# Two RMS norms between two transformer blocks, folded into one scale per token that is applied behind the projections

## The chip, the cores and the metric

One core of a Trainium2 chip (trn2). The program computes two layers in one launch; the metric is the device time of that launch in microseconds, as the median of several runs. Inputs are in the chip's memory in layouts that the host made ahead; the output is a 256 x 1024 array of float32.

## The reference, cut to what matters

```python
# end of the first block, with x of shape (256, 1024)
x = x + conv_glu_ffn(rms_norm(x, ffn_norm_g), w_up, ffn_conv_w, w_down)
x = rms_norm(x, final_norm_g)                  # first norm between the blocks
...
# start of the second block: 16 meta tokens stand ahead of the 256
xn = rmsnorm(concat([meta_tokens, x]), norm1_g)   # second norm
proj = xn @ w_in_2                             # 12 column blocks first: 8 for xm, 4 for the state space branch
xm -> causal conv of 4 taps -> silu -> block diagonal q, k;  xm -> block diagonal v
...
x = x + mixer output                           # the residual is the output of the first norm
```

Both norms are y = x * rsqrt(mean(x^2) + eps) * g, over the 1024 channels of a token. x is kept transposed: 128 partitions hold channels, 8 tiles k of 128 channels each, tokens are the columns (256, or 272 with the meta tokens).

## The kernel before, in words

The kernel is written straight for the engines: every engine has its own program, a stage is a block with a barrier of all engines at its end, and semaphores order the work inside a block. Weights come as a stream of 512 KB pieces (128 partitions x 1024) that SyncE loads into a ring of 8 slots; a slot is loaded again once TensorE has told `used` for it.

**Split products.** The projections in question run in three passes of a fast format. ScalarE rounds a ring slot to its high part (`part_high`, L247 to L249), VectorE subtracts that from the slot and leaves the low part in the slot's place (`part_low`, L251 to L254), and TensorE multiplies high by high, high by low and low by high (`three`, L256 to L260). The activations are split in the same way. A product of one 128-column block is 8 x 3 matmuls of 272 tokens.

**The stages around the change**, in order:

1. The feed-forward block (L1022 to L1173). Banks 0 to 3 of PSUM gather x plus the down projection. At its end VectorE waits for TensorE's last product (L1120), copies the four banks to x (L1122), and the block ends.
2. `rms_norm` of x with final_norm_g into `xin` (L1182). ScalarE squares four tiles and VectorE the other four, VectorE adds them in pairs, TensorE sums over the partitions with a matrix of ones (L288, 4 matmuls), VectorE makes mean + eps and its reciprocal (L305, L307), ScalarE the root (L282), VectorE scales the 8 tiles (L310).
3. `rms_norm` of xin, now with the 16 meta tokens, into `h` (L1193). The same steps again; beside it ScalarE rounds the first three ring slots.
4. The large block of the second layer (L1274 on). ScalarE rounds h in two halves (L1543), VectorE subtracts (L1332) and then makes the low parts of the slots; TensorE runs the 12 products (L1648) in banks 0 to 3, in turn; ScalarE copies each out of its bank (L1547) and rounds the slot three ahead (L1546); from the fifth slot on VectorE also runs the 4-tap convolution of a finished tile after each low part (`conv`, L1319 to L1327: 4 linked operations). Then TensorE goes on with plain float32 projections of h (`z_products`, L1249, one of 8 matmuls each, in banks 0 and 1 at first), the block diagonal products (L1655 to L1671) and the heads; VectorE goes on with the state space parameters (from L1342), which need exp(log_dt) from ScalarE (L1552), the heads and the scans. GpSimd clears `k0` (L1292), copies xin to x for the residual (L1293) and later multiplies in eight rounds, one per scan pair (L1301 to L1305). The block ends with 6 plain projections (L1785) on TensorE.

Each engine works in its own program order: a wait in VectorE's list holds all that stands behind it.

Of the kernel before, what the change touches and what calls it, by code (L numbers as in the profile page):

```python
# [104 lines left out]
def build(nc, out, stream, x_t, meta_t, cols, first, second, last, keep):  # L105
    with ExitStack() as ctx:
# [28 lines left out]
        spare = sb("spare", [P, 1])  # L135
        arena, arena_parts = split_place("arena", [P, 38912], ARENA_PARTS)
# [126 lines left out]
        normed = {"n": 0}  # L263

        def rms_norm(src, dst, gain, eps, squares, width=T, beside=None):


            n = normed["n"]
            normed["n"] += 1
            sq, total, mean, root = S("norm_squares"), S("norm_total"), S("norm_mean"), S("norm_root")  # L270
            with nc.Block() as block:
# [13 lines left out]
                def _(pe):  # L285
                    for k in range(4):
                        pe.wait_ge(sq, n * 4 + k + 1)
                        mm = nc.tensor.matmul(bank[7][:, 0:width], ones, squares[:, 4 + k, 0:width],  # L288
                                              start=k == 0, stop=k == 3)
# [698 lines left out]
        xin = a6.take(KT, TT)  # L988
        sq2 = a6.take(KT, TT)
# [24 lines left out]
        def ff_low(dve, n, i=0):  # L1014
# [6 lines left out]
                 beside=(lambda act: [ff_high(act, n) for n in (-4, -3)], lambda dve: [ff_low(dve, n) for n in (-4, -3)]))  # L1021
        with nc.Block() as block:  # L1022
            @block.sync
            def _(sp):
                sp.dma_start(xin[:, :, 0:M], meta_t).then_inc(S("meta_in"), 16)
# [52 lines left out]
            def _(dve):  # L1078
# [41 lines left out]
                dve.wait_ge(used[FF_LAST[1]], before[FF_LAST[1]] + 1)  # L1120
                for b in range(4):
                    ins = v.tensor_copy(x[:, 2 * b:2 * b + 2, :], b3(b))  # L1122
                    ins.then_inc(drained[b], 1)
                for b in range(4):
                    dve.wait_ge(drained[b], pe_at.banks[b] + 2)

            @block.scalar
            def _(act):
# [17 lines left out]
                for j in range(2):  # L1146
                    silu(pairs, j)

# [36 lines left out]
        xp = Area(arena_parts[25344])  # L1185
        xn_block, xn_high, xn_low = xp.take(4, D), xp.take(KT, TT), xp.take(KT, TT)
        xn_filled = [pe_at.rounds[s] + 1 for s in range(4)]

        def xn_part_high(act, n, i=0):
            if not (isinstance(i, int) and i * 4 + n >= 12):  # L1190
                part_high(act, xn_block, n % 4, i + (n // 4 + xn_filled[n % 4]))

        rms_norm(lambda k: xin[:, k, :], lambda k: h[:, k, :], "norm1_g_2", RMS_EPS, squares_b, TT,  # L1193
# [1398 lines left out]
```

## Time and profile before

| | us |
|---|---|
| median of 3 runs (lowest, highest) | 1820.93 (1820.82, 1825.67) |
| the profiled execution's own time | 1822.69 |
| its span | 1820.9 |
| mean granted TensorE clock, share of full speed | 0.956 |

Times in rows are microseconds from the start of the span, unless marked ns. PE is TensorE's matmuls, PEld its weight loads, DVE VectorE, ACT ScalarE, POOL GpSimd; L12 is line 12 of the kernel. A float32 matmul in full precision leaves two matmul records in the trace, one of the fast format leaves one.

### The profile page before, as it was taken

To read this page: it belongs to the slowest core of one execution; us is meant where nothing else is said; L and a number is where in the kernel's file an instruction comes from. 1 tells how busy PE (TensorE), PEld (TensorE's weight loads), DVE (VectorE), ACT (ScalarE), POOL (GpSimd) and SP (SyncE) were. 2 spreads that over 40 slices of the span, in tenths; PEclk is the share of its full clock that TensorE was granted. 3 is DMA by queue.
4 is the path that set the end of the run, shared out by engine and by line. 5 is a ranking of instruction groups with operands and counts; after the bars stand their busy time and mean duration, and the time that the engine had idled before them with its cause. 6 is when DMAs were issued, how large, how long until landed. Compare 5 with 4: busy or idle time off the path is not lost. (4 is left out here: it accounts for less than half of the span.)

```text
span 1820.9 us, 32801 instructions
## 1 busy us (share of the span) xinstructions
PE 1677.4 (92%) x11170; PEld 1517.9 (83%) x11170; DVE 1152.2 (63%) x2268; ACT 794.7 (44%) x1326; POOL 333.6 (18%) x205
## 2 busy tenths in 40 slices
PE   5989898779999499999969998999999999999997
PEld 4968897669999396777859998999999988888886
DVE  4464312847676674662445999777775477777776
ACT  3441112225553265223324554455555555555554
POOL 0030000404444000221727697000000000000000
PEclk8989899889999699899979999999999999999999
DMA  6403123324554141114434667555556776666663
GB/s 229 175 24 104 58 82 127 117 90 178 185 186 171 62 172 70 35 47 150 155 100 137 202 217 204 169 175 174 178 178 205 237 235 238 232 232 233 237 232 127
DMA packets 93700, 289.44 MB, mean 159 GB/s; under 512 B 11328, under 2 KB 27968, under 8 KB 93248
## 3 DMA queue, kind: packets, MB, share of 16 engines
q1 hardware_dynamic: 93200, 287.61, 46.2%
q10 hardware_dynamic: 432, 0.90, 0.2%
q8 instruction: 45, 0.74, 0.2%
q14 instruction: 23, 0.19, 0.0%
HBM read 270.64 MB, written 17.83 MB: 158 GB/s over the span
## 5 line engine op out<-in xcount | busy, mean ns | idle before, releaser
L258 PE MATMUL psum<-arena_parts 128*128 128x256 f32 (+2 forms) x1664 | 483.3, 290 | 59.9 <-DVE ring_parts L253 24.1
L260 PE MATMUL psum<-arena_parts,ring_parts 128*128 128x256 f32 (+1 forms) x1600 | 455.6, 285 | 0.0
L2380 DVE TENSOR_TENSOR ring_parts<-ring,arena_parts 128x512 fp32r<-128x512 f32 x434 | 293.4, 689 | 132.4 <-ACT arena_parts L2200 104.6
L258 PEld LDWEIGHTS psum<-arena_parts 128*128 128x128 f32 x1664 | 320.8, 193 | 64.3 <-issue 29.0
L259 PE MATMUL psum<-h_parts,arena_parts 128*128 128x256 f32 x1152 | 325.2, 282 | 0.0
L260 PEld LDWEIGHTS psum<-arena_parts,ring_parts 128*128 128x128 f32 x1600 | 308.5, 193 | 0.0
L253 POOL TENSOR_TENSOR ring_parts<-ring,arena_parts 128x1024 fp32r<-128x1024 f32 x79 | 208.5, 2655 | 319.6 <-ACT arena_parts L249 265.6
L259 PEld LDWEIGHTS psum<-h_parts,arena_parts 128*128 128x128 f32 x1152 | 219.4, 190 | 0.0
L229 PE MATMUL psum<-h,ring 128*128 128x256 f32 x896 | 212.2, 397 | 0.0
L2169 PE MATMUL psum<-arena_parts,x_parts 128*128 128x512 f32 x512 | 202.9, 396 | 2.7 <-DVE x_parts L2407 2.7
L2171 PE MATMUL psum<-arena_parts,x_parts 128*128 128x512 f32 x512 | 202.7, 396 | 0.0
L2170 PE MATMUL psum<-ring_parts,x_parts 128*128 128x512 f32 x512 | 200.9, 392 | 0.0
L229 PEld LDWEIGHTS psum<-h,ring 128*128 128x128 f32 x896 | 176.2, 200 | 28.9 <-issue 2.7
L2200 ACT ACTIVATE arena_parts<-ring 128x512 fp32r<-128x512 f32 x217 | 136.4, 629 | 124.1 <-PE psum L2171 96.8
L2197 ACT ACTIVATE arena_parts<-ring 128x512 fp32r<-128x512 f32 x217 | 136.6, 630 | 76.1 <-PE psum L2171 58.8
L259 PE MATMUL psum<-arena_parts 128*128 128x256 f32 (+1 forms) x448 | 130.3, 291 | 0.0
L2169 PEld LDWEIGHTS psum<-arena_parts,x_parts 128*128 128x128 f32 x512 | 95.7, 187 | 25.9 <-DVE ring_parts L2380 2.9
L1017 DVE TENSOR_TENSOR ring_parts<-ring,arena_parts 128x1024 fp32r<-128x1024 f32 x66 | 84.0, 1277 | 52.6 <-ACT arena_parts L1012 47.9
L2170 PEld LDWEIGHTS psum<-ring_parts,x_parts 128*128 128x128 f32 x512 | 96.3, 188 | 23.5
L2171 PEld LDWEIGHTS psum<-arena_parts,x_parts 128*128 128x128 f32 x512 | 95.7, 187 | 24.1
L249 ACT ACTIVATE arena_parts<-ring 128x1024 fp32r<-128x1024 f32 x76 | 79.3, 1053 | 56.1 <-DMA ring<-stream 56.0
L1051 PE MATMUL psum<-arena_parts 128*128 128x256 f32 x352 | 100.2, 285 | 2.8 <-DVEq L1101 2.8
(486 smaller groups left out, 2903.1 us busy)
## 6 DMA issues: line engine op xcount, KB each, us to landing
ring<-stream SPq DMA_DIRECT2D x473, 512.0 KB, 3.6
kept<-arena SPq DMA_DIRECT2D x128, 128.0 KB, 2.0
arena<-kept SPq DMA_DIRECT2D x32, 512.0 KB, 4.7
arena<-first SPq DMA_DIRECT2D x1, 2144.0 KB, 7.7
arena<-second SPq DMA_DIRECT2D x1, 1632.0 KB, 7.1
x<-x_t SPq DMA_DIRECT2D x1, 1024.0 KB, 5.8
out<-arena SPq DMA_DIRECT2D x4, 256.0 KB, 2.1
arena<-last ACTq DMA_DIRECT2D x1, 512.0 KB, 3.4
```

The source lines that it names most:

```text
L229: mm = nc.tensor.matmul(b[:, 0:width], w[:, k, :], h[:, k, lo:lo + width], start=k == 0, stop=k == KT - 1)
L253: ns.tensor_tensor(low[:, s, :], ring[:, s, :], high[:, s, :].bitcast(F32), ALU.subtract)\
L258: nc.tensor.matmul(dst, stationary[0], moving[0], start=first, stop=False)
L259: nc.tensor.matmul(dst, stationary[0], moving[1], start=False, stop=False)
L260: return nc.tensor.matmul(dst, stationary[1], moving[0], start=False, stop=last_one)
L1051: mm(b, high[:, s, w], h_high[:, k, :], start=k == 0, stop=False)
L2169: mm(b, gate_high[:, q % 4, t], expert_high[:, m % 2, w], start=False, stop=False)
L2170: mm(b, gate_high[:, q % 4, t], low[:, s, w], start=False, stop=False)
L2171: ins = mm(b, gate_low[:, q % 4, t], expert_high[:, m % 2, w], start=False, stop=last_one)
L2197: nc.scalar.activation(expert_high[:, m % 2, halves[0]], ring[:, s, halves[0]], ACT.Copy)\
L2200: nc.scalar.activation(expert_high[:, m % 2, halves[1]], ring[:, s, halves[1]], ACT.Copy)\
L2380: v.tensor_tensor(low[:, s, w], ring[:, s, w], expert_high[:, m % 2, w].bitcast(F32), ALU.subtract)\
```

## The change

- The feed-forward block no longer waits for the last product on VectorE and copies nothing out. In its place VectorE prepares small tables: `both_g` = final_norm_g * norm1_g, the meta tokens times norm1_g, their squares, and `sums_of`, a stationary matrix per tile whose left 64 columns are final_norm_g^2 + eps and whose right 64 columns are ones; ScalarE and VectorE split the first three ring slots there.
- Both calls of `rms_norm` are gone. In the large block ScalarE makes the high part of x * both_g straight from the PSUM banks and VectorE the low part, bank by bank; the first product waits for each bank's parts (tiles 0 and 1, then 2 and 3, ...).
- Behind that VectorE copies the banks to x, ScalarE squares x (4 operations), and after the third product TensorE sums the squares: 8 matmuls of 16 columns for the meta tokens, 8 of 256 columns with `sums_of`. Rows 0 to 63 of the sum give the joint scale of both norms, rows 64 to 127 that of the first norm alone. VectorE and ScalarE make the inverse root once, TensorE spreads row 0 over all partitions (one matmul, after the fourth product), ScalarE copies it to `scale`.
- The products run in seven banks (4, 5, 6, 0, 1, 2, 3, ...). VectorE takes each out of its bank times `scale` (`take`), in an order written out by hand among the low parts and convolutions; 8 operations that write the scaled h stand behind the last low part. Before the first plain projection TensorE waits for these 8.
- The residual is scaled late: one more matmul spreads row 64 (`scale_1`), ScalarE copies it, and GpSimd multiplies x by it and by final_norm_g, 16 operations behind its eight rounds.

```diff
@@ the feed-forward block, VectorE @@
-                dve.wait_ge(used[FF_LAST[1]], before[FF_LAST[1]] + 1)
-                for b in range(4):
-                    ins = v.tensor_copy(x[:, 2 * b:2 * b + 2, :], b3(b))
-                    ins.then_inc(drained[b], 1)
-                for b in range(4):
-                    dve.wait_ge(drained[b], pe_at.banks[b] + 2)
+                gain_1, gain_2 = (par[:, at[n]:at[n] + KT] for n in ("final_norm_g", "norm1_g_2"))
+                dve.wait_ge(S("meta_in"), 16)
+                v.tensor_tensor(both_g, gain_1, gain_2, ALU.mult)
+                v.tensor_tensor(meta_g, meta, gain_2.unsqueeze(2).broadcast_to([P, KT, M]), ALU.mult)
+                v.tensor_tensor(meta_squares, meta, meta, ALU.mult)
+                vec.link(v.tensor_tensor(both_square, gain_1, gain_1, ALU.mult))
+                vec.link(v.tensor_scalar(both_square, both_square, RMS_EPS, None, ALU.add))
+                v.tensor_copy(sums_of[:, :, 0:64], both_square.unsqueeze(2).broadcast_to([P, KT, 64]))
+                v.tensor_copy(sums_of[:, :, 64:P], ones[:, 0:64].unsqueeze(1).broadcast_to([P, KT, 64]))
+                v.memset(eps_row[0:64, :], RMS_EPS * RMS_EPS)
+                v.memset(eps_row[64:P, :], RMS_EPS)
+                for n in range(AHEAD):
+                    part_low(dve, nc.vector, xn_block, n, split["blocks"] + 3 * FT + n + 1)
@@ ScalarE @@
+                for n in range(AHEAD):
+                    xn_part_high(act, n)
@@ between the blocks @@
-        rms_norm(lambda k: x[:, k, :], lambda k: xin[:, k, M:TT], "final_norm_g", RMS_EPS, squares_b := sq2)
-        rms_norm(lambda k: xin[:, k, :], lambda k: h[:, k, :], "norm1_g_2", RMS_EPS, squares_b, TT, ...)
@@ the large block, GpSimd @@
-                poo.tell(g.tensor_copy(x[:], xin[:, :, M:TT]), x_kept, ONCE + 1)
...
+                pool.wait_ge(k0_ready, ONCE + 1)
+                for k in range(KT):
+                    ins = g.tensor_tensor(x[:, k, :], x[:, k, :], scale_1[:], ALU.mult)
+                poo.link(ins)
+                for k in range(KT):
+                    ins = g.tensor_scalar(x[:, k, :], x[:, k, :], col("final_norm_g", k), None, ALU.mult)
+                poo.link(ins)
@@ VectorE @@
+                def take(n):
+                    evacuate(dve, [n % 4], [P_BANKS[n]], 1, lambda q, b, i: v.tensor_tensor(
+                        both[:, n, :], b[:, 0:TT], scale[:, 0:TT], ALU.mult))
...
+                for b in range(4):
+                    dve.wait_ge(S("h_rounded"), split["h"] + b + 1)
+                    if b == 0:
+                        v.tensor_tensor(xn_low[:, :, 0:M], meta_g, xn_high[:, :, 0:M].bitcast(F32), ALU.subtract)
+                    for k in (2 * b, 2 * b + 1):
+                        ins = v.scalar_tensor_tensor(xn_low[:, k, M:TT], x_half(k), both_g[:, k:k + 1],
+                                                     xn_high[:, k, M:TT].bitcast(F32), ALU.mult, ALU.subtract)
+                    ins.then_inc(S("h_parts"), 1)
+                for b in range(4):
+                    v.tensor_copy(x[:, 2 * b:2 * b + 2, :], b3(b)).then_inc(drained[b], 1)
+                next_low(3); next_low(4)
+                dve.wait_ge(S("norm_total"), n_norm + 1)
+                v.tensor_scalar(roots[:, 0:M], bank[7][:, 0:M], 1.0 / D, RMS_EPS, ALU.mult, ALU.add)
+                vec.link(v.tensor_scalar(roots[:, M:TT], bank[7][:, M:TT], 1.0 / D, eps_row, ALU.mult, ALU.add))
+                vec.tell(v.reciprocal(roots[:], roots[:]), S("norm_mean"), n_norm + 1)
+                next_low(5)
+                dve.wait_ge(scales_made, ONCE + 1)
+                take(0);  next_low(6);  conv(0)
+                take(1);  next_low(7);  conv(1)
+                take(2);  next_low(8)
+                take(3);  conv(2);  next_low(9)
+                take(4);  conv(3);  next_low(10)
+                take(5);  next_low(11)
+                for k in range(KT):
+                    ins = v.scalar_tensor_tensor(h[:, k, M:TT], x[:, k, :], both_g[:, k:k + 1], scale[:, M:TT],
+                                                 ALU.mult, ALU.mult)
+                ins.then_inc(h_scaled, 1)
+                take(6);  conv(4);  take(7);  conv(5);  take(8);  take(9)
+                conv(6);  take(10);  take(11);  conv(7)
@@ ScalarE @@
-                for n in range(12):
-                    if n + AHEAD < 12:
-                        xn_part_high(act, n + AHEAD)
-                    evacuate(act, [n % 4], [n % 4], 1, lambda q, b, i: a.activation(both[:, n, :], b[:, 0:TT], ACT.Copy))
-                    if n >= 6:
-                        silu(n - 6)
+                a.activation(xn_high[:, :, 0:M], meta_g, ACT.Copy)
+                for k in range(KT):
+                    ins = a.activation(xn_high[:, k, M:TT], bank[k // 2][:, k % 2 * T:(k % 2 + 1) * T], ACT.Identity,
+                                       scale=both_g[:, k:k + 1])
+                    if k % 2:
+                        ins.then_inc(S("h_rounded"), 1)
+                xn_part_high(act, 3)
+                for b in range(4):
+                    act.wait_ge(drained[b], free_at[b])
+                    ins = a.activation(x_squares[:, 2 * b:2 * b + 2, :], x[:, 2 * b:2 * b + 2, :], ACT.Square)
+                    if b % 2:
+                        ins.then_inc(S("norm_squares"), 1)
+                xn_part_high(act, 4)
+                a.activation(spare[:], ones[:, 0:1], ACT.Sqrt)
+                act.wait_ge(S("norm_mean"), n_norm + 1)
+                a.activation(roots[:], roots[:], ACT.Sqrt).then_inc(S("norm_root"), 1)
+                xn_part_high(act, 5)
+                act.wait_ge(scale_spread, ONCE + 1)
+                sca.tell(a.activation(scale[:, 0:TT], bank[7][:, 0:TT], ACT.Copy), scales_made, ONCE + 1)
+                for n in range(6, 12):
+                    xn_part_high(act, n)
+                    if n >= 8:
+                        silu(n - 8)
+                for c in range(4, 6):
+                    silu(c)
@@ TensorE @@
-                    project(pe, [n % 4], [n % 4], 1, product(n))
+                    project(pe, [n % 4], [P_BANKS[n]], 1, product(n))
+                    if n == 2:
+                        for k in range(KT):
+                            mm(bank[7][:, 0:M], ones, meta_squares[:, k, :], start=k == 0, stop=k == KT - 1)
+                        for k in range(KT):
+                            if k % 4 == 0:
+                                pe.wait_ge(S("norm_squares"), normed["squares"] + k // 4 + 1)
+                            ins = mm(bank[7][:, M:TT], sums_of[:, k, :], x_squares[:, k, :], start=k == 0, stop=k == KT - 1)
+                        ins.then_inc(S("norm_total"), 1)
+                    if n == 3:
+                        pe.wait_ge(S("norm_root"), n_norm + 1)
+                        mm(bank[7][:, 0:TT], ident[:, 0:1].broadcast_to([P, P]), roots[:], start=True, stop=True)\
+                            .then_inc(scale_spread, 1)
...
+                pe.wait_ge(h_scaled, ONCE + 1)
                 z_products(pe, 2)
...
+                mm(bank[4][:, T:2 * T], ident[:, 64:65].broadcast_to([P, P]), roots[:, M:TT], start=True, stop=True)
```

In the diff above, calls of one line that stand under each other in VectorE's list are written side by side.

## Rows read from the trace of the kernel before

**Rows 1.** The page: busy time of each engine, share of the span, instructions.
```profile
PE 1677.4 (92%) x11170; PEld 1517.9 (83%) x11170; DVE 1152.2 (63%) x2268; ACT 794.7 (44%) x1326; POOL 333.6 (18%) x205
```
**Rows 2.** Timeline of TensorE: start, duration, line, shapes, count, [idle before <-releaser].
```profile
589.96 0.28 PE L1065 MATMUL psum<-arena_parts,ring_parts 128*128 128x256 f32 x1
...
624.51 0.57 PE L258 MATMUL psum<-arena_parts 128*128 128x272 f32 x1 [12.79 <-DVE ring_parts L253]
...
662.32 7.07 PE L229 MATMUL psum<-h,ring 128*128 128x256 f32 x32
...
836.29 14.08 PE L229 MATMUL psum<-h,ring 128*128 128x256 f32 x64
```
**Rows 3.** Timeline of VectorE between the two blocks.
```profile
590.27 2.48 DVE L1122 COPY x<-psum 128x512 f32<-128x512 f32 x4 [6.21 <-PE psum L1065]
593.39 1.43 DVE L296 TENSOR_TENSOR arena<-x 128x256 f32<-128x256 f32 x4 [0.64 <-PEq L1022]
...
601.92 3.26 DVE L310 SCALAR_TENSOR_TENSOR arena<-x,par,scale 128x256 f32<-128x256 f32 x8 [0.55 <-ACT scale L282]
...
612.23 1.85 DVE L307 RECIPROCAL scale<-scale 128x272 f32<-128x272 f32 x1
...
623.15 4.62 DVE L253 TENSOR_TENSOR ring_parts<-ring,arena_parts 128x1024 fp32r<-128x1024 f32 x4
```
**Rows 4.** Timeline of ScalarE from the feed-forward block's end to the first reload.
```profile
584.15 0.42 ACT L1131 ACTIVATE arena<-arena 128x256 f32<-128x256 f32 x1 [3.53 <-DVEq L1101]
...
614.12 0.43 ACT L282 ACTIVATE scale<-scale 128x272 f32<-128x272 f32 x1 [4.12 <-DVE scale L307]
...
629.66 0.40 ACT L1547 ACTIVATE arena<-psum 128x272 f32<-128x272 f32 x1 [8.06 <-PE psum L260]
633.41 1.06 ACT L249 ACTIVATE arena_parts<-ring 128x1024 fp32r<-128x1024 f32 x1 [3.35 <-DMA ring<-stream]
```
**Rows 5.** Windows: length; busy PE, PEld, DVE, ACT, POOL; clock; DMA; GB/s.
```profile
624.50:626.50 2.00, 1.99 (x9) 2.00 (x10) 2.00 (x2) 0.00 (x0) 0.00 (x0) 0.50 0.02 7
...
630.50:662.00 31.50, 31.50 (x255) 31.50 (x255) 24.47 (x40) 14.54 (x24) 0.00 (x0) 1.00 0.63 227
```
**Rows 6.** Timeline of TensorE: two other short stops in the program.
```profile
353.58 0.58 PE L258 MATMUL psum<-arena_parts 128*128 128x256 f32 x1 [2.41 <-DVE arena_parts L976]
...
871.78 3.72 PE L1821 MATMUL psum<-arena,ring 128*128 128x256 f32 x16 [2.26 <-DVE arena L1880]
```
**Rows 7.** Timeline of TensorE: small float32 matmuls of the large block.
```profile
716.48 1.95 PE L1697 MATMUL psum<-cst,arena 128*128 128x128 f32 x16
```
**Rows 8.** Timeline of VectorE: convolution, low part, a product read from PSUM.
```profile
645.25 0.41 DVE L1321 TENSOR_SCALAR arena<-arena,par 128x272 f32<-128x272 f32 x1
645.70 1.57 DVE L1325 SCALAR_TENSOR_TENSOR arena<-arena,par 128x271 f32<-128x271 f32 x3
647.31 1.22 DVE L253 TENSOR_TENSOR ring_parts<-ring,arena_parts 128x1024 fp32r<-128x1024 f32 x1
...
821.15 0.44 DVE L1449 TENSOR_TENSOR arena<-psum,arena 128x272 f32<-128x272 f32 x1 [1.84 <-PE psum L1725]
```
**Rows 9.** Timelines: VectorE's first parameter operation, TensorE's stop before the heads.
```profile
664.86 0.18 DVE L1342 TENSOR_TENSOR arena<-par,arena 128x16 f32<-128x16 f32 x1 [4.79 <-ACT arena L1552]
...
720.21 0.73 PE L1708 MATMUL psum<-cst,arena 4*16 4x4 f32 x6 [0.99 <-DVE arena L1426]
```
**Rows 10.** Timeline of GpSimd: its last operation of the large block.
```profile
828.64 0.73 POOL L1305 TENSOR_TENSOR arena<-arena 128x258 f32<-128x258 f32 x1
```
**Rows 11.** Groups of GpSimd by line and shape: busy, mean ns | idle before.
```profile
L1301 POOL TENSOR_TENSOR arena<-arena 128x258 f32<-128x258 f32 x8 | 5.9, 732 | 176.7 <-DVE arena L1468 167.1 <-issue 9.7
L509 POOL TENSOR_SCALAR arena<-arena,par 128x256 f32<-128x256 f32 x4 | 4.4, 1090 | 0.4
L506 POOL TENSOR_TENSOR arena<-arena 128x256 f32<-128x256 f32 x2 | 3.9, 1931 | 107.2 <-POOLq L359 107.1
```
**Rows 12.** One line of GpSimd: durations in ns, min/median/max, first and last start.
```profile
L1160 POOL TENSOR_TENSOR arena<-arena x22: 731/1105/1387, 413.2 to 584.6; 128x256 f32<-128x256 f32 x22
```

More of the change, by code:

```diff
@@ L1181, in build @@
                     tiles.banks[b] += 1
-        rms_norm(lambda k: x[:, k, :], lambda k: xin[:, k, M:TT], "final_norm_g", RMS_EPS, squares_b := sq2)
[L1185 to L1193, printed above, removed]
-                 beside=(lambda act: [xn_part_high(act, n) for n in range(AHEAD)], lambda dve: None))
+        n_norm = normed["n"]
+        normed["n"] += 1
         a7 = Area(arena, a6.at)
@@ L1216, in build @@
         k0 = r1.take(4, P)
-        assert r1.at <= a6.at
+        x_squares = Area(arena, 18560).take(8, T)
+        P_BANKS = (4, 5, 6, 0, 1, 2, 3, 4, 5, 6, 0, 1)
+        both = arena[:, a6.at:a6.at + 12 * TT].rearrange("p (c t) -> p c t", t=TT)
+        assert r1.at <= 4992
         a8 = Area(arena, a7.at)
@@ L1270, in build @@
         bt_re, bt_im = (bt[:, n, :].rearrange("p (c n) -> p c n", c=4) for n in range(2))
-        free_at = [ev_at.banks[n] + 1 for n in range(4)]
+        free_at = [ev_at.banks[n] + 1 for n in range(7)]
         projected = pe_at.rounds[3] + 3
+        k0_zeroed = poo.n + 1
         with nc.Block() as block:
@@ L1327, in conv, with x_half @@
                         vec.link(ins) if back < 3 else vec.tell(ins, S("ml_conv"), c + 1)
-                for half in range(2):
-                    k = slice(4 * half, 4 * half + 4)
-                    dve.wait_ge(S("h_rounded"), split["h"] + half + 1)
-                    v.tensor_tensor(xn_low[:, k, :], h[:, k, :], xn_high[:, k, :].bitcast(F32), ALU.subtract)\
-                        .then_inc(S("h_parts"), 1)
-                for n in range(12):
-                    part_low(dve, nc.vector, xn_block, n % 4, split["blocks"] + n + 1)
-                    if n >= 4:
-                        conv(n - 4)
+                def x_half(k):
+                    return bank[k // 2][:, k % 2 * T:(k % 2 + 1) * T]
@@ new lines, in _ @@
+                next_low(5)
+                dve.wait_ge(scales_made, ONCE + 1)
+                take(0)
+                next_low(6)
+                conv(0)
+                take(1)
+                next_low(7)
+                conv(1)
+                take(2)
+                next_low(8)
+                take(3)
+                conv(2)
+                next_low(9)
+                take(4)
+                conv(3)
+                next_low(10)
+                take(5)
+                next_low(11)
```

64 lines of the change are left out of this document (44 added, 20 removed).

## The prediction

> **What bounds the kernel now.** The page gives TensorE 92% of the span [rows 1], so the question is where it stands still, and the timeline of TensorE is read first. Its last product of the feed-forward block starts at 589.96 and lasts 0.28 us, so it ends at 590.24; the first product of the next block starts at 624.51 [rows 2]. In these 34.3 us TensorE has only the two norms' sums to do. VectorE's timeline shows what fills them: the copies out of PSUM, the squares and their additions, each norm's reciprocal, its 8 scalings, and the low parts [rows 3]. After 624.51 TensorE is fully busy: the window from 630.5 to 662 is 31.5 us of 31.5 at the full clock of 2.4 GHz [rows 5], and the first plain projection starts at 662.32 [rows 2]. From there to the heads its largest stop is 0.99 us [rows 9]. So the stretch from 590.24 to 662.32, 72.1 us, is what the change can shorten; what follows should move with its end if the other engines move along.
>
> The sum is made against the profiled execution: span 1820.9 us, own time 1822.69 us. That is 1.8 us above the median of 1820.93, and I subtract the saving from the median.
>
> **The change, part by part.** I build the same stretch anew, on the clock of the old trace.
>
> *Feed-forward tail.* VectorE was idle for 6.21 us before 590.27 [rows 3], from 584.06. Its new tables are 10 small operations, about 2 us by rows of 0.18 (16 columns) to 0.44 us (272 columns) [rows 8, 9], and three low parts at 4.62 / 4 = 1.15 us [rows 3]: done at 584.1 + 2 + 3.5 = 589.6. ScalarE is free at 584.57 [rows 4] and rounds three slots at 1.06 us [rows 4] by 587.8. Both are under TensorE's last products, with 0.6 us to spare on VectorE; without that cover they would cost their 5.5 us. The barrier took 0.64 us [rows 3]: 590.9.
>
> *First parts.* ScalarE: the meta tokens (0.25 us, under the 0.40 of 272 columns [rows 4]) and two tiles at 0.36 us: 591.9. VectorE: meta 0.25, two tiles at 0.41 us (3.26 / 8 [rows 3]), a handover of 0.1: 593.1. TensorE starts there, 31.4 us earlier than before. Later banks come every 0.85 us, six matmuls at the half clock of 1.2 GHz take 1.36 us (0.5 in the windows, 9 matmuls in 2 us [rows 5]), so the parts keep ahead.
>
> *The clock.* The old first product took from 624.51 to 629.66, when ScalarE read it [rows 2, 4]: 5.1 us, against 31.5 x 24 / 255 = 2.97 us for a warm one [rows 5]. A cold start costs 2.1 us. After a stop of 2.9 us either can be: a stop of 2.41 us was followed by a cold matmul of 0.58 us, one of 2.26 us by sixteen warm ones in 3.72 us [rows 6]. I take cold: product 0 ends at 598.2, products 1 and 2 at 604.1.
>
> *Sums.* 8 full float32 matmuls of 256 columns cost 7.07 / 4 / 4 x 8 = 3.54 us, since the 32 records of [rows 2] are 16 matmuls. The 8 of 16 columns lie between 0.2 us (by columns alone, a sixteenth of 3.54) and 1.95 us, what 16 records with full stationary tiles and 128 columns took [rows 7]; I take 1.5, since loading the tiles stays: 609.2. The copies of x (2.48 us [rows 3]) and the squares end by 600, under products 1 and 2.
>
> *Root.* VectorE: 0.6 us for the mean in two pieces, 1.85 for the reciprocal [rows 3]: 611.7. Root 0.43 us [rows 4]: 612.1, when product 3 ends too. The spread costs TensorE 0.5 us, ScalarE rounds slot 5 (1.06 us) and copies the scale (0.4). VectorE is idle until slot 5 is rounded at 613.2; products 4 to 6 run meanwhile in free banks.
>
> *VectorE behind it.* Here is what the change adds to the bound. ScalarE used to empty the banks at 0.40 us each [rows 4]; now VectorE does, behind the scale. Before TensorE may start the first plain projection in bank 0, `take(10)` must be done, and ahead of it stand, without a pause: 7 low parts x 1.15 = 8.05; 11 takes x 0.42 (0.44 for the same shape [rows 8], a little less back to back) = 4.6; 7 convolutions x 2.05 (645.25 to 647.31 [rows 8]) = 14.35; 8 scalings of h x 0.41 = 3.3. Together 30.3 us: 643.5. TensorE alone would be done with product 11 at 612.6 + 8 x 2.97 = 636.4. So it stops for 7 us, and the first plain projection, cold again, loses another 2 us, since nothing waits for VectorE's rest more than before: `conv(7)` ends 2.5 us after TensorE's start, and the parameters used to begin at 664.86, 2.54 us after 662.32 [rows 2, 9]. The effective start is 645.5, a gain of 16.8 us.
>
> A price by a page: the Trainium skill, VectorE: DVE Perf Modes, section "The TRN2 errata", charges a VectorE operation from PSUM 62 cycles more than one from SBUF; as an estimate that adds 0.7 us for 11 takes, and the result would be 0.7 us later. The trace prices the PSUM form directly, at 0.44 us [rows 8], and that is used.
>
> *Reloads.* A low part needs its slot loaded again. Product 0 was read at 629.66, the next load rounded from 633.41 [rows 4]: 3.75 us, plus 1.06 and 1.15 for the two parts, 6 us in all, while three other products take 9 us. VectorE comes to each low part later than its load. Cost nothing; a load late by more than 3 us would hold the takes behind it.
>
> *Later.* `scale_1` costs TensorE 0.44 us and ScalarE 0.36 us, the latter under a plain projection. ScalarE is rid of 12 copies, GpSimd of its copy of x, neither on the path. GpSimd's 16 operations follow its last round, which ended at 829.37 [rows 10]; TensorE ended at 836.29 + 14.08 = 850.37 [rows 2]. So 21.0 us are free. By 0.73 us for products and 1.09 us for operations with a pointer [rows 11] they take 14.6 us: hidden.
>
> Sum: 16.8 - 0.4 = 16.4 us, 1820.93 - 16.4 = **1804.5 us**.
>
> **The rivals.**
>
> *A, TensorE bound after all.* If VectorE needed 7 us less than 30.3, TensorE would run through from product 11: another 7 + 2 us, 1795.5. Against it: every term has a row of its own, and a quarter of them would have to be wrong. Chance 0.07.
>
> *B, same path, warm starts.* If the clock holds over the 2.9 us stop (2.1 us) the end comes at 1802.4; with cheap meta sums (1.3 us) at 1801. Both outcomes stand in [rows 6]. Chance 0.22.
>
> *C, GpSimd's tail sets the block's end.* Its product took 731 to 1387 ns [rows 12], the slow ones beside VectorE's low parts, and 1931 ns elsewhere [rows 11]. Sixteen at 1.8 us are 28.8, 7.8 us over the 21.0: 1812.3. At 1.93 they are 30.9, 9.9 over: 1814.4. It decides from 1.31 us each on. Against it: VectorE is nearly idle in these 21 us. Chance 0.08. The Trainium skill has a rule for it, GPSIMD Engine Reference, section "Key points": GpSimd shares its SBUF interfaces with VectorE, and contends with instructions of two SBUF inputs. By that rule the tail would be slow only next to such work; the spread in [rows 12] agrees, but no row shows this tail.
>
> *D, slower than before.* The same place: if a GpSimd operation there cost over (21.0 + 16.4) / 16 = 2.34 us, the tail would be longer than slack and gain together; at 3 us each, 48 us, the time is 1820.9 - 16.4 + 27 = 1831.5. It needs more than any such row of 256 columns. Chance 0.03.
>
> *E, little change.* VectorE's list is held by a chain that I have as hidden: a slot that is reloaded late holds all takes behind it. With four late loads of 3 to 4 us each 12 to 16 us are lost: 1816.5 to 1820.5. Against it are the 3 us of slack at each. Chance 0.05.
>
> **How the numbers follow.** The forecast path has 0.55, and with B 0.77. The predicted time is the forecast's, 1804.5. Its own bounds: 2.1 + 1.3 + 2.0 us (both starts warm, cheap meta sums) better is 1799.1; 10% more on VectorE's 30.3, with 0.7 for waits between, 3.7 us worse, is 1808.2. C reaches to 1812.3 at the nearer price. The range 1799.5 to 1812.5 leaves out A, D, E and the rest of C. A run can tell 0.3% (5.5 us) from no change, so faster means under 1815.5: the forecast, A, B and C, 0.92. Same: E, 0.05. Slower: D, 0.03.
>
> **What would show it.** Right: TensorE's gap at 590 shrinks to some 3 us; VectorE is busy without a pause from about 613 to 645; TensorE stops for about 7 us before its first plain projection, released by VectorE's `take`; that projection starts near 644 at half clock; the parameters follow 2 to 3 us later; GpSimd ends before TensorE in the block. Wrong: a wait of the first product for later than 594, a stop among products 4 to 9, a VectorE wait for ScalarE or a load in that stretch, the block's end waiting for GpSimd, or new stops of TensorE after 650.

## The result, and the profile of the changed kernel

| | before | changed |
|---|---|---|
| median | 1822.59 us (4 runs, 1820.82 to 1825.67) | 1806.76 us (4 runs, 1803.80 to 1809.51) |
| the profiled execution's own time | 1822.69 us | 1803.80 us |
| its span | 1820.9 us | 1802.0 us |

The ratio is 0.9906, with a 95% interval of 0.9891 to 0.9922: about 17 us saved (the two medians lie 15.8 us apart). The forecast was 16.4 us, at 1804.5 us; it started from 1820.93 us, the median of three runs, and a fourth run of before has moved that to 1822.59.

Line numbers have moved: the rounding of a slot is now L250, its low part L254, the three passes of a split product L259 to L261, a plain projection L230.

TensorE first, the row that answers to the 624.51 and 662.32 of [rows 2], and what lies between them.

```profile
593.28 0.28 PE L1079 MATMUL psum<-arena_parts,ring_parts 128*128 128x256 f32 x1
596.85 0.56 PE L259 MATMUL psum<-arena_parts 128*128 128x272 f32 x1 [3.29 <-DVE arena_parts L1372]
...
607.46 1.85 PE L1745 MATMUL psum<-arena,cst 128*128 128x16 f32 x16
609.17 3.70 PE L1749 MATMUL psum<-arena 128*128 128x256 f32 x16
612.52 0.47 PE L259 MATMUL psum<-arena_parts 128*128 128x272 f32 x1
...
615.88 0.72 PE L1753 MATMUL psum<-roots,cst 128*128 128x272 f32 x2
...
646.65 9.51 PE L230 MATMUL psum<-h,ring 128*128 128x256 f32 x32 [6.05 <-DVE arena L1360]
...
703.26 1.95 PE L1803 MATMUL psum<-cst,arena 128*128 128x128 f32 x16
705.04 0.60 PE L1806 MATMUL psum<-roots,cst 128*128 128x256 f32 x2
...
706.98 0.73 PE L1815 MATMUL psum<-cst,arena 4*16 4x4 f32 x6 [0.56 <-DVE arena L1503]
...
818.61 20.99 PE L230 MATMUL psum<-h,ring 128*128 128x256 f32 x96
```

The stop of 34.3 us is 3.3 us. A new stop of 6.05 us stands ahead of the first plain projection, and L1360 is `take`. The two projections behind it take 9.51 us where they took 7.07 [rows 2]: the granted clock is 0.50 for their first 4.5 us and 1.00 from 651.65 us on.

VectorE in the same stretch: its work in the feed-forward tail, the split out of PSUM, the mean, and the list behind it.

```profile
587.46 0.17 DVE L1136 TENSOR_TENSOR arena<-par 128x8 f32<-128x8 f32 x1 [0.15 <-DVE arena L1111]
...
588.90 0.85 DVE L1141 COPY arena<-arena 128x512 f32<-128x512 f32 x1
589.67 0.96 DVE L1142 COPY arena<-cst 128x512 f32<-128x512 f32 x1
...
590.75 3.50 DVE L254 TENSOR_TENSOR ring_parts<-ring,arena_parts 128x1024 fp32r<-128x1024 f32 x3
595.62 0.29 DVE L1370 TENSOR_TENSOR arena_parts<-arena,arena_parts 128x128 fp32r<-128x128 f32 x1 [1.38 <-ACT arena_parts L1618]
595.83 3.22 DVE L1372 SCALAR_TENSOR_TENSOR arena_parts<-psum,arena,arena_parts 128x256 fp32r<-128x256 f32 x8
...
613.51 1.85 DVE L1382 RECIPROCAL roots<-roots 128x272 f32<-128x272 f32 x1
616.89 1.23 DVE L254 TENSOR_TENSOR ring_parts<-ring,arena_parts 128x1024 fp32r<-128x1024 f32 x1 [1.52 <-ACT arena_parts L250]
618.03 0.43 DVE L1360 TENSOR_TENSOR arena<-psum,scale 128x272 f32<-128x272 f32 x1
...
646.07 0.79 DVE L1360 TENSOR_TENSOR arena<-psum,scale 128x272 f32<-128x272 f32 x2
646.77 0.41 DVE L1346 TENSOR_SCALAR arena<-arena,par 128x272 f32<-128x272 f32 x1
647.22 1.57 DVE L1350 SCALAR_TENSOR_TENSOR arena<-arena,par 128x271 f32<-128x271 f32 x3
648.83 0.17 DVE L1419 TENSOR_TENSOR arena<-par,arena 128x16 f32<-128x16 f32 x1
```

Behind 616.89 no row of VectorE up to 648.83 has an idle mark: its list is what TensorE waits for. `take(10)` is the first of the two at 646.07. The parameters begin at 648.83, 2.2 us behind TensorE's 646.65; before it was 2.5 us [rows 2, 9].

GpSimd's tail: first its last round, then the 16 operations.

```profile
810.97 1.01 POOL L1322 TENSOR_TENSOR arena<-arena 128x258 f32<-128x258 f32 x1
812.06 5.94 POOL L1325 TENSOR_TENSOR x<-x,scale 128x256 f32<-128x256 f32 x8
818.11 7.22 POOL L1328 TENSOR_SCALAR x<-x,par 128x256 f32<-128x256 f32 x8
```

It ends at 825.33, 14.3 us before the end of TensorE's last projections, 818.61 + 20.99 = 839.60.

**A measure that chance touches less.** Single runs of one kernel differ by 5 us and more, so the runs below are compared by a stretch of TensorE as well: from the end of the last feed-forward product (its start plus 0.28 us, or the next row's start less its idle mark) to the small transposes ahead of the heads (L1708 before, L1815 changed), a point with a wait for VectorE in every profile. It repeats within 0.6 us: 129.5 to 130.1 us in three profiles without the change, 113.4 and 113.9 in two of the changed kernel. Each variant has one profile. Before: 720.21 - 590.24 = 129.97 us. Changed: 706.98 - 593.56 = 113.42 us, 16.6 us less. In the table "stretch" is this. The runs were made in groups, each beside runs of before whose median lay between 1822.59 and 1825.46 us; the ratio is taken inside a group, the medians of different groups are less comparable. Where the intervals of two ratios overlap, as those of the clock held, the longer tail, the copy first and the tables late do with the changed kernel's, the whole time does not tell the two apart, and the reading rests on the stretch or on a stop.

| run | median, us | ratio to before, 95% | stretch, us |
|---|---|---|---|
| before | 1822.59 | | 129.97 |
| changed | 1806.76 | 0.9906 (0.9891 to 0.9922) | 113.42 |
| changed, again | 1807.74 | 0.9909 (0.9894 to 0.9925) | 710.78 - 596.86 = 113.92 |
| takes first | 1799.24 | 0.9858 (0.9843 to 0.9873) | 701.10 - 594.83 = 106.27 |
| clock held | 1803.46 | 0.9894 (0.9878 to 0.9911) | 703.71 - 593.53 = 110.18 |
| longer tail | 1811.16 | 0.9928 (0.9913 to 0.9943) | 706.85 - 593.02 = 113.83 |
| copy first | 1806.24 | 0.9907 (0.9892 to 0.9921) | 706.72 - 592.37 = 114.35 |
| four banks | 1811.48 | 0.9937 (0.9926 to 0.9949) | 709.66 - 592.52 = 117.14 |
| tables late | 1808.42 | 0.9912 (0.9899 to 0.9926) | 708.19 - 595.51 = 112.68 |
| combination | 1797.36 | 0.9852 (0.9837 to 0.9866) | 699.96 - 595.96 = 104.00 |
| combination, tables early | 1794.43 | 0.9833 (0.9816 to 0.9850) | 698.84 - 594.24 = 104.60 |
| before, again (one run) | 1820.95 | | 721.38 - 591.85 = 129.53 |
| before, moved | 1823.20 | 1.0003 (0.9987 to 1.0019) | 722.66 - 592.57 = 130.09 |

### The profile page after: what moved, and what is told of

It reads as the page before. It is cut to its first block and busy times, and to the rows that moved or that the text cites. A ratio compares the mean times of both kernels' runs of the same rounds, so it can differ in the third digit from the quotient of the medians.

```text
span 1802.0 us, 32825 instructions
## 1 busy us (share of the span) xinstructions
PE 1673.4 (93%) x11190; PEld 1517.6 (84%) x11190; DVE 1150.8 (64%) x2271; ACT 793.3 (44%) x1317; POOL 345.2 (19%) x220
## 5 line engine op out<-in xcount | busy, mean ns | idle before, releaser
L259 PE MATMUL psum<-arena_parts 128*128 128x256 f32 (+2 forms) x1664 | 483.7, 291 | 51.3 <-DVE h_parts L2414 13.3
L261 PE MATMUL psum<-arena_parts,ring_parts 128*128 128x256 f32 (+1 forms) x1600 | 455.2, 284 | 0.0
L259 PEld LDWEIGHTS psum<-arena_parts 128*128 128x128 f32 x1664 | 320.6, 193 | 55.4 <-issue 18.8
L261 PEld LDWEIGHTS psum<-arena_parts,ring_parts 128*128 128x128 f32 x1600 | 309.1, 193 | 0.0
L254 POOL TENSOR_TENSOR ring_parts<-ring,arena_parts 128x1024 fp32r<-128x1024 f32 x79 | 208.3, 2652 | 309.5 <-ACT arena_parts L250 255.2
L230 PE MATMUL psum<-h,ring 128*128 128x256 f32 x896 | 209.6, 393 | 6.0 <-DVE arena L1360 6.0
L230 PEld LDWEIGHTS psum<-h,ring 128*128 128x128 f32 x896 | 174.6, 198 | 34.1 <-issue 9.1
L250 ACT ACTIVATE arena_parts<-ring 128x1024 fp32r<-128x1024 f32 x76 | 79.5, 1056 | 54.7 <-DMA ring<-stream 54.7
```

The lines of the kernel that those rows point to most:

```text
L230: mm = nc.tensor.matmul(b[:, 0:width], w[:, k, :], h[:, k, lo:lo + width], start=k == 0, stop=k == KT - 1)
L254: ns.tensor_tensor(low[:, s, :], ring[:, s, :], high[:, s, :].bitcast(F32), ALU.subtract)\
L259: nc.tensor.matmul(dst, stationary[0], moving[0], start=first, stop=False)
L261: return nc.tensor.matmul(dst, stationary[1], moving[0], start=False, stop=last_one)
```

## The experiments

Theory: the saving is the closed stop (34.3 - 3.3 = 31.0 us), less TensorE's own new work (612.52 - 607.46 = 5.1 us for the sums, some 0.5 us for the spread), less the stop in which it waits for VectorE's list (6.05), less one more start at half clock (2.4; product 0 started so before as well). That leaves some 17 us; the rest is hidden. Rivals: the list only hides a later bound; banks, clock or GpSimd's tail carry the time.

**The changed kernel again**, without an edit.

> The changed kernel once more, for a firmer ratio. Forecast: 16 us under the kernel before (ratio 0.991); TensorE's stop before the first plain projection 6 us, released by VectorE's take. If the earlier gain of the heads section (4.5 us in one profile, where TensorE's clock fell to half less often) were a part of the change, that section would again be 4 us shorter than before in this profile; if it is chance of the clock, it is between the two.

Measured: 0.9909, and a stop of 6.29 us released by `take`:

```profile
650.18 9.77 PE L230 MATMUL psum<-h,ring 128*128 128x256 f32 x32 [6.29 <-DVE arena L1360]
```

The heads section, from L1815 to the next block's first product, takes 850.56 - 710.78 = 139.8 us here, against 843.01 - 706.98 = 136.0 in the first profile of the changed kernel and 860.69 - 720.21 = 140.5 before. It is not 4 us shorter again. What differs is the clock: windows of 1 us over the section show stretches of some 4 us at half clock, four before, one in the first changed profile, three in this one (two of them back to back). In the mean of the section:

```profile
720.20:860.70 140.50, 136.00 (x695) 106.82 (x695) 70.14 (x159) 34.94 (x56) 29.24 (x40) 0.95 0.19 70
```

for the kernel before, and for the first profile of the changed one

```profile
707.00:843.00 136.00, 131.04 (x694) 103.38 (x695) 71.04 (x159) 35.16 (x57) 42.72 (x56) 0.99 0.20 72
```

The same number of matmuls, up to one missing record, the granted clock 0.95 against 0.99 (third column from the right).

**Takes first.** VectorE's list only (calls that stand under each other are written side by side):

```diff
-                take(6);  conv(4);  take(7);  conv(5);  take(8);  take(9)
-                conv(6);  take(10);  take(11);  conv(7)
+                take(6);  take(7);  take(8);  take(9);  take(10);  take(11)
+                conv(4);  conv(5);  conv(6);  conv(7)
```

> VectorE does take(6) to take(11) in a row, then conv(4) to conv(7). Theory (VectorE's list is the bound of the stretch, three convolutions stand ahead of the take that TensorE waits for): the stop of 6.05 us goes, the first plain projections run warm (7.1 in place of 9.5 us), conv(7) still ends at its old time, and nothing later waits for it: 8 us faster than the changed kernel. Rival (the parameters behind the convolutions are as critical, so that the stop moves to a later place): 0 to 3 us faster, with a new wait of TensorE for VectorE or ScalarE before the heads.

Measured: 8.5 us faster than the changed kernel run beside it, and the intervals of the two ratios do not touch; the stretch is 7.65 us shorter (106.27 against 113.92; 7.15 against the first profile). TensorE in this run:

```profile
641.72 7.07 PE L230 MATMUL psum<-h,ring 128*128 128x256 f32 x32
...
651.84 2.10 PE L1762 MATMUL psum<-arena,ring 128*128 128x272 f32 x8 [1.22 <-ACT arena L1609]
...
701.10 0.73 PE L1815 MATMUL psum<-cst,arena 4*16 4x4 f32 x6 [0.56 <-DVE arena L1503]
```

No idle mark ahead of the plain projection. The wait ahead of the heads is 0.56 us as before the edit, though the parameters now follow the first projection by 8.8 us (VectorE's L1419 at 650.53) in place of 2.2: they were not critical. The one new wait, 1.22 us, is for ScalarE, which has two silus ahead of its reads. The theory holds; of the rival only this wait is left.

**Clock held.** TensorE's list:

```diff
+                for _ in range(12):
+                    mm(bank[7][:, 0:P], ones, ident, start=True, stop=True)
                 for n in range(12):
...
+                for _ in range(22):
+                    mm(bank[7][:, 0:P], ones, ident, start=True, stop=True)
                 pe.wait_ge(h_scaled, ONCE + 1)
```

> 12 small float32 matmuls (128 columns, into bank 7, results unused) before product 0 and 22 after product 11, in place of TensorE's two stops. They take 2.9 and 5.3 us. Theory (the cold clock costs 1.7 to 2.1 us after the first stop and 2.4 us after the second): product 0 takes 3.3 us in place of 5.1, two plain projections 7.1 us in place of 9.5, the total 4 us less. Rival (after the first stop VectorE's parts pace product 0, after the second VectorE is late again): 0 to 2 us less.

Measured: 4.3 us less than the changed kernel beside it in the median, 3.2 to 3.7 us in the stretch. Both places, in this run:

```profile
594.55 2.92 PE L1742 MATMUL psum<-cst 128*128 128x128 f32 x24 [1.02 <-PEq L1036]
...
597.22 0.37 PE L259 MATMUL psum<-arena_parts 128*128 128x272 f32 x1
...
606.31 1.86 PE L1747 MATMUL psum<-arena,cst 128*128 128x16 f32 x16
...
645.74 7.14 PE L230 MATMUL psum<-h,ring 128*128 128x256 f32 x32 [1.37 <-DVE arena L1360]
```

From product 0 to the sums it takes 606.31 - 597.22 = 9.09 us against 607.46 - 596.85 = 10.61: 1.5 us. But the 12 small matmuls lasted too long: product 0 starts 597.22 - 593.53 = 3.69 us after the feed-forward products in place of 3.29, so 1.1 us are left at this place. The first two plain projections take 7.14 us against 9.51: 2.4 us. The window over product 0, first in the changed kernel, then in this run, shows the half clock that the small matmuls avoid:

```profile
596.90:600.30 3.40, 3.40 (x15) 3.40 (x16) 3.40 (x9) 2.44 (x6) 0.00 (x0) 0.51 0.91 380
```

```profile
596.90:600.30 3.40, 3.40 (x30) 3.40 (x29) 3.40 (x9) 2.45 (x6) 0.00 (x0) 1.00 0.93 392
```

Theory right on both, the first by less than priced (1.7 to 2.1 us).

**Longer tail.** GpSimd, between its two groups of 8:

```diff
+                for _ in range(4):
+                    for k in range(KT):
+                        ins = g.tensor_tensor(x[:, k, :].rearrange("p (a t) -> p a t", a=2), x[:, k, :].rearrange("p (a t) -> p a t", a=2),
+                                              ones.unsqueeze(1).broadcast_to([P, 2, P]), ALU.mult)
+                    poo.link(ins)
```

> 32 more multiplications by one on GpSimd (8 tiles, four times) in its tail. At 0.74 us each they are 23.7 us; the tail of 13.3 us ended 14.3 us before TensorE did. Theory (hidden tail with 14.3 us of slack): GpSimd sets the block's end and the total grows by 9 us. Rival (no slack, the tail is on the path): 24 us more. Second rival (nothing waits for it at the block's end): no change.

Measured: 1811.16 us, 3.4 us over the changed kernel. GpSimd and TensorE of this run:

```profile
819.62 22.28 POOL L1329 TENSOR_TENSOR x<-x,cst 128x256 f32<-128x256 f32 x32
842.00 7.22 POOL L1333 TENSOR_SCALAR x<-x,par 128x256 f32<-128x256 f32 x8
```

```profile
849.88 8.75 PE L1934 MATMUL psum<-arena,ring 128*128 128x256 f32 x32 [7.64 <-PEq L1292]
```

GpSimd does set the end now: it ends at 849.22 and TensorE starts 0.66 us later. But the stop between the blocks grew by 7.64 - 3.41 = 4.2 us, not 9. The slack was taken against TensorE; the block's end without the longer tail is set by ScalarE, whose last operation, the gelu, ends 2.8 us after TensorE:

```profile
843.97 1.06 ACT L1717 ACTIVATE arena<-arena 128x1024 f32<-128x1024 f32 x1
```

849.22 - 845.03 = 4.2 us. The longer tail added 842.00 - 819.62 = 22.4 us, so the true slack of the tail is 22.4 - 4.2 = 18.2 us in this profile. The mechanism holds. Of the 3.9 us by which the slack was set too small (14.3), 2.8 are ScalarE's share; the other 1.1 us come from the profile, in which TensorE's last projections lie later against GpSimd's tail.

**Copy first.** The split reads x behind the copies in place of PSUM ahead of them; first VectorE's part, then ScalarE's.

```diff
+                for b in range(4):
+                    v.tensor_copy(x[:, 2 * b:2 * b + 2, :], b3(b)).then_inc(drained[b], 1)
...
-                        ins = v.scalar_tensor_tensor(xn_low[:, k, M:TT], x_half(k), both_g[:, k:k + 1],
+                        ins = v.scalar_tensor_tensor(xn_low[:, k, M:TT], x[:, k, :], both_g[:, k:k + 1],
...
-                for b in range(4):
-                    v.tensor_copy(x[:, 2 * b:2 * b + 2, :], b3(b)).then_inc(drained[b], 1)
...
-                    ins = a.activation(xn_high[:, k, M:TT], bank[k // 2][:, k % 2 * T:(k % 2 + 1) * T], ACT.Identity,
+                    if k % 2 == 0:
+                        act.wait_ge(drained[k // 2], free_at[k // 2])
+                    ins = a.activation(xn_high[:, k, M:TT], x[:, k, :], ACT.Identity,
```

> The split out of PSUM undone: VectorE copies the banks to x first (2.5 us), and both parts are made from x. Theory (this part is worth the time by which TensorE's first product comes earlier): product 0 starts 4.5 us after the feed-forward products end in place of 3.2 us, since ScalarE works beside the copies, and the total grows by 1 to 1.5 us. Rival (the short stop is what matters most in this change): 2.5 us or more. Either way most of the gain over the kernel before stays.

Measured: product 0 starts 4.64 us after the feed-forward products, 1.35 us later than in the changed kernel; the stretch is 0.4 to 0.9 us longer, less than the 1 to 1.5 us of the theory, and the medians cannot tell the two apart. The split straight out of PSUM, one part of the change, is worth 1 us at most by the stretch; of the 2.5 us of copies 1.35 stood ahead of product 0, the rest beside ScalarE.

**Four banks.**

```diff
-        P_BANKS = (4, 5, 6, 0, 1, 2, 3, 4, 5, 6, 0, 1)
+        P_BANKS = (0, 1, 2, 3) * 3
```

> The products use banks 0 to 3 in turn, as the kernel before did, in place of seven banks. Product 0 then waits for the copy of bank 0 (2.9 us later), product 4 for take(0). Theory (the three spare banks only cover the wait for the scale; VectorE's list of 30 us stays the bound): 3 to 4 us slower than the changed kernel, TensorE's stop is spread over products 4 to 11 in place of standing ahead of the plain projection. Rival (the banks carry the gain): over 8 us slower.

Measured: 3.7 us slower in the median (5.1 us by the ratios), 3.2 to 3.7 in the stretch. Product 0 waits 6.19 us for the copy, products 4, 5, 6, 9 and 10 wait 1.96, 0.30, 0.30, 0.73 and 2.54 us, and the stop ahead of the plain projection is gone: VectorE's list is paid for in other places. Theory right.

**Tables late.** `meta_squares`, `both_square`, `sums_of` and `eps_row` move behind `next_low(3)`, with a semaphore that TensorE awaits before the sums (the lines between the first and the last of the tables move along).

```diff
-                v.tensor_tensor(meta_squares, meta, meta, ALU.mult)
...
-                v.memset(eps_row[64:P, :], RMS_EPS)
...
+                v.tensor_tensor(meta_squares, meta, meta, ALU.mult)
...
+                v.memset(eps_row[64:P, :], RMS_EPS).then_inc(S("tables_made"), 1)
...
+                        pe.wait_ge(S("tables_made"), 1)
```

> The tables that only the sums need (meta squares, sums_of, eps rows; 2.9 us of VectorE) move from the feed-forward tail to behind the low part of slot 3, where VectorE waits 3.8 us. Theory (in the tail VectorE's last low part ended 0.7 us after TensorE's last product, so the cover that was forecast failed by that): the first stop shrinks from 3.2 to 2.5 us, the total by 0.7 us. Rival (it makes the sums late): TensorE waits for them ahead of the sums, no gain.

Measured: no gain in the median (1808.42). The first stop did shrink, to 2.60 us, but a new one of 0.88 us stands ahead of TensorE's last feed-forward product, released by GpSimd:

```profile
592.44 0.35 PE L1077 MATMUL psum<-arena_parts 128*128 128x256 f32 x1 [0.88 <-POOL arena_parts L1182]
```

```profile
589.89 0.73 POOL L1178 TENSOR_TENSOR arena_parts<-arena,cst 128x256 fp32r<-128x256 f32 x1
590.71 1.59 POOL L1182 TENSOR_TENSOR arena_parts<-arena,arena_parts 128x256 fp32r<-128x256 f32 x1
```

GpSimd's last split takes 1.59 us beside VectorE's low parts, in this run and in the combination; beside the tables it took 0.80 or 0.81 in the other eight profiles with the change. VectorE's three low parts take 4.54 us here and 3.50 with the tables ahead of them. The split at 589.89 overlaps the first low part, which starts 0.09 us after it, and takes 0.73 us all the same: what in a pair of operations decides is not shown. Neither case of the expectation: the time came back on another engine.

**The combination.** Takes first, tables late, 6 small matmuls ahead of product 0, and on ScalarE (`z_reads` copies the plain projections out of their banks):

```diff
-                for c in range(4, 6):
-                    silu(c)
+                silu(4)
+                z_reads(act, 1)
+                silu(5)
                 sca.tell(a.activation(sm(S_DT), ldt, ACT.Exp), S("s5_dt"))
+                z_reads(act, 1)
                 for c in (6, 7):
                     silu(c)
-                z_reads(act, 2)
```

> Takes first, tables late, 6 small matmuls ahead of product 0 to hold the clock, and ScalarE reads the first plain projections out before its last two silus (in the run with the takes first TensorE waited 1.2 us for that). Theory: 8.5 + 0.7 + 2 + 1.2 us, 12 us under the changed kernel. Rival (the gains overlap, since TensorE becomes the bound of the stretch and VectorE's parameters follow late): 9 us.

Measured: 1797.36 us, 10.4 us under the changed kernel's second median and by the ratios; the stretch is 104.00 us, 9.4 to 9.9 us under the changed kernel, and 0.9 us of that stand as GpSimd's stop just ahead of it. That is nearer the rival's 9 than 12. TensorE still waits 1.04 us for ScalarE at the same product as in the run with the takes first, where it was 1.22, so ScalarE's new order took 0.2 us off that wait and did not remove it:

```profile
650.70 2.10 PE L1768 MATMUL psum<-arena,ring 128*128 128x272 f32 x8 [1.04 <-ACT arena L1611]
```

**The combination with the tables in the tail**, where the changed kernel has them, and 8 small matmuls:

```diff
-                for _ in range(6):
+                for _ in range(8):
                     mm(bank[7][:, 0:P], ones, ident, start=True, stop=True)
```

> The fastest combination, but with the tables back in the feed-forward tail and 8 small matmuls ahead of product 0. Theory (tables in the tail delay the stage's end by 0.7 us, tables late let the three low parts run beside GpSimd's last split and delay TensorE's last product by 0.9 us, so the two cancel): the same time as the combination within 0.5 us from the end of the feed-forward block on, and no stop of TensorE for GpSimd at its last product. Rival (only the late tables gave the last 2 us): 2 us slower, as the run with the takes first.

Measured: 1794.43 us, ratio 0.9833 (0.9816 to 0.9850). The stretch is 104.60 us against 104.00 + 0.89 = 104.9 for the combination with its new stop counted in: within 0.3 us, and there is no stop for GpSimd. This is the lowest median of all. It is 3 us under the combination, which the stretch does not explain and which the overlapping intervals of the ratios do not show; the heads sections of the two profiles, 137.2 and 140.5 us, show how much the clock alone moves.

**The kernel before, twice.** Once as it is, once with the change's two new tensors, unused, so that the arena moves:

```diff
+        roots, scale_1 = sb("roots", [P, TT]), sb("scale_1", [P, T])
```

> The kernel before, for a second profile. In the changed kernel and its variants the feed-forward block ended at 592.4 to 596.9 us, in the one profile of the kernel before at 590.2, though nothing was edited ahead of it. Theory (chance, by the clock of TensorE in the small stages ahead): this profile lies anywhere from 590 to 597. Rival (the change made the stages ahead 3 us slower, for one by the new tensors that move the arena in SBUF): again 590 to 591. The heads section, 116.1 us from its first wait to the last six projections, should vary as well: 111 to 117 us.

> The kernel before with the two new tensors of the change, unused, so that the arena lies where the change has it. Theory (addresses cost nothing): the time of the kernel before within 3 us, the feed-forward block ends at 590 to 597 us. Rival (the place in SBUF costs 3 us ahead of the feed-forward block's end): 3 us slower, an end at 593 or later in this and in no profile of the unmoved kernel.

Measured: stretches of 129.5 and 130.1 us; the moved kernel has a ratio of 1.0003 (0.9987 to 1.0019). No cost of the new addresses shows, to within 3 us, and with an end of the feed-forward block at 592.6 us the rival of the second expectation falls. The feed-forward block ends at 590.2, 591.9 and 592.6 us in the three profiles without the change, at 592.4 to 596.9 in the ten with it (the 0.9 us of GpSimd is in two of them). The ranges nearly meet, but on average the stages ahead, in which no instruction was edited, are some 2.5 us later in the changed kernel. The heads sections were 140.5 us in all three profiles of before, alike to 0.01 us and each with four stretches at half clock. In the ten others (the wait for the longer tail taken out) they were 136.0 to 140.5 with one to four such stretches, 2.3 us shorter on average. The two differences nearly cancel. The second goes with the clock; why both lean one way stays open.

## Why the prediction was right, step by step

The terms of the sum, put on the changed profile's clock (3.3 us later at the start):

| step | forecast | measured |
|---|---|---|
| stop ahead of product 0 | 2.9 us | 3.29 us |
| product 0 | 5.1 us | 601.46 - 596.85 = 4.6 us |
| products 0 to 2 | 11.0 us | 607.46 - 596.85 = 10.6 us |
| 8 small sums, 8 full sums | 1.5 and 3.5 us | 1.85 and 3.70 us, overlapping |
| reciprocal ends | 611.7 + 3.3 = 615.0 | 615.36 |
| VectorE's list begins | 613.2 + 3.3 = 616.5 | 616.89 |
| the list up to take(10) | 30.3 us | 29.6 us |
| plain projection starts | 643.5 + 3.3 = 646.8 | 646.65 |
| stop ahead of it | 7 us | 6.05 us |
| cold clock behind it | 2 us | 9.51 - 7.07 = 2.4 us |
| stretch | 16.4 us less | 16.6 and 16.1 us less |

- *The bound.* VectorE's list, not TensorE, ended the wait ahead of the plain projections, as worked out. The run with the takes first shows it as a cause: three convolutions moved, 8.5 us gained.
- *The tail of the feed-forward block.* This step was wrong by a little. VectorE was to be done 0.6 us before TensorE; it was done 0.7 us after it, at 594.25 against 593.56. The tables took 3.3 us in place of 2: the two copies of 512 elements took 0.85 and 0.96 us beside GpSimd, 0.43 and 0.42 us without it (the run with the tables late), and one product of 8 elements 0.71 us against 0.16. Without GpSimd beside them the nine operations (the forecast counted ten) took 0.36 + 1.47 = 1.8 us in that run, so the term was right for VectorE alone, and the sum had left GpSimd out. The rest of the first stop was shorter than priced, so the stop came out 0.4 us over.
- *GpSimd's tail* was priced at 14.6 us and took 13.3 us, hidden. But its slack was misread: the row at 836.29 was cut at the edge of the stretch it was read in. The six last projections are 96 records and end at 857.28, not 850.37, and the block ends with ScalarE's gelu after that. The whole row is

```profile
836.29 20.99 PE L229 MATMUL psum<-h,ring 128*128 128x256 f32 x96
```

The slack against TensorE was thus 27.9 us, not 21.0; rivals C and D were further off than their prices said. The forecast did not suffer, since the term stayed hidden either way.
- *Reloads.* No wait of VectorE between 616.89 and 648.83: hidden, as said.
- *`scale_1`* was priced at 0.4 us and cost nothing. Its matmul (L1806) lies inside the stretch, just ahead of the wait at L1815: that wait shrank from 0.99 to 0.56 us, and from the 16 small matmuls ahead to the transposes it takes 706.98 - 703.26 = 3.72 us, before 720.21 - 716.48 = 3.73. The path up to the plain projections came out 0.3 us longer than forecast (53.09 + 2.44 us, against 53.3 + 2.0), and this 0.4 us too much covers it: that the stretch agrees to 0.2 us is in part luck.
- *Rivals.* A (TensorE bound) did not come by itself; it took another order on VectorE. B, the warm start, came in no profile without small matmuls ahead of product 0: products 0 to 2 took 10.4 us or more in each. In two of them (the changed kernel again, the longer tail) the clock was still full at product 0 and fell to half some 0.7 us into it, which cost the same. Forcing the full clock took 1.5 us off the products. The cheap meta sums of B did not come either: 1.85 us. C, D and E did not come.
- *The PSUM surcharge.* The Trainium skill, VectorE: DVE Perf Modes, section "The TRN2 errata", would have added 0.7 us for 11 takes. The takes took 0.43 to 0.44 us, and VectorE's products of the same shape with both inputs in SBUF took 0.43 us in the kernel before (731.64 us, L1454): by this trace no surcharge shows.
- *The shared port.* The rule of the Trainium skill, GPSIMD Engine Reference, section "Key points", that GpSimd contends with VectorE instructions that have two SBUF inputs or run in a two-port mode, was held against the tail, where nothing came of it. In the feed-forward tail, where I had not looked, the trace agrees: 0.81 against 1.59 us for GpSimd's last split beside VectorE's low parts, which have two inputs. VectorE's copies, 0.43 against 0.85 and 0.96 us, have one input, and no row shows their mode. Of the 22 operations of [rows 12] 20 ran beside a low part, at 0.74 to 1.39 us: the slow ones did, as the prediction has it, but so did the fast ones.

## What to carry to other kernels

When a serial chain is taken off the bound engine's path, write out what then stands in the in-order list of the engine that takes over its last step, and put ahead only what the bound engine waits for: here three convolutions in the wrong place cost half as much as the whole change gained. A slack is measured to the last engine at the barrier, and a row that touches a window's edge may be cut. Where work is added under cover, look at what runs beside it: here VectorE's tables and GpSimd's splits lengthened each other.

## What the runs showed that I had not expected

- Taking the tables out ahead of VectorE's three low parts brought these beside GpSimd's last split. That lengthened one GpSimd operation from 0.81 to 1.59 us and so stopped TensorE for 0.88 us.
- In a section whose instructions on TensorE do not change, and in which it is busy nearly throughout, TensorE's clock fell to half between one and four times, and the section took 136.0 to 140.5 us: about 1.5 us for each time. That is over a quarter of what this change gained, and nearly as large as the spread of single runs.
- Behind the same stop of 2.26 us in the next block, TensorE went on at full clock in nine profiles (3.72 us for 16 records, where the row is whole) and at half clock in four (5.3 to 5.4 us: takes first, clock held, both combinations). What decides between the two is not shown.
- Small matmuls with unused results, 12 ahead of the products and 22 ahead of the projections, made the stretch 3 to 4 us shorter by holding the clock.
